# The last stage's matmuls on pairs of fp16 parts instead of pairs of fp32r parts, in one layer of a hybrid attention backbone

## What is computed

```python
def _merge(x, oa, za, ob, zb, ga, gb, gate, w_br_a, w_br_b, w_out):
    ya = (oa * jax.nn.silu(za)) @ w_br_a
    yb = (ob * jax.nn.silu(zb)) @ w_br_b
    h = jax.nn.sigmoid(ga) * ya + jax.nn.sigmoid(gb) * yb
    return x + gate * (h @ w_out)
# and, for both groups of tokens: y = rmsnorm(_merge(...)) * gain
```

## Time and profile before

| | before |
|---|---|
| median of three runs (lowest, highest) | 1109.42 us (1109.13, 1110.87) |
| the profiled execution, its own time | 1108.12 us |
| its span, first to last instruction | 1106.0 us |
| mean granted TensorE clock | 0.996 |
| PE busy / PE weight loads / DVE / ACT / POOL, share of the span | 96% / 85% / 69% / 50% / 9% |
| last stage, PE's last 1106.0 - 881 us | 225 us |

### The profile page before, as it was taken

The page is one execution under the profiler, slowest core; times in us unless marked ns, Lnnn a source line. Parts: engine busy times, 40 slices in busy tenths (PEclk is TensorE's granted clock), DMA queues, the critical chain, the costliest instruction groups (busy, mean ns, idle before and its releaser), DMA issues.

```text
span 1106.0 us, 18405 instructions
## 1 busy us (share of the span) xinstructions
PE 1063.2 (96%) x6515; PEld 941.7 (85%) x6515; DVE 768.0 (69%) x1538; ACT 555.5 (50%) x1036; POOL 104.9 (9%) x115
## 2 busy tenths in 40 slices
PE   5999999999999999998999999989999899999997
PEld 4899888988988898888888888778887789899896
DVE  3669577867876786776788688688688776445443
ACT  4552347645653664565577477377466542212111
POOL 0000200000000000000000000000000165352430
PEclk9999999999999999999999999999999999999999
DMA  9826637964974797399498498669769995353530
GB/s 372 327 84 178 199 88 149 184 189 87 183 160 134 158 190 187 73 192 213 140 184 169 95 177 175 145 138 184 164 144 210 259 337 196 104 195 108 191 134 38
DMA packets 318862, 188.98 MB, mean 171 GB/s; under 512 B 255926, under 2 KB 298934, under 8 KB 317756
## 3 DMA queue, kind: packets, MB, share of 16 engines
q1 hardware_dynamic: 304812, 165.90, 62.0%
q10 hardware_dynamic: 13968, 22.03, 6.0%
HBM read 94.27 MB, written 32.78 MB: 115 GB/s over the span
## 4 chain that ended last, share of the span: by engine, by line
PE 62%; DVE 15%; DMA 8%; ACT 6%; SPq 6%; issue 4%; DVEq 0%; ACTq 0%
PE d_ps_pairs L108 15%; PE y_ps L2157 10%; PE s_ps_pairs L108 10%; PE b_ps L108 10%; PE o_ps_pairs L998 5%; PE v_ps L108 4%; SPq L1130 4%; DMA xl<-pl 4%; DVE pl L1698 4%; DVE mn L1621 3%; ACT pr L1384 2%; DMA xh<-ph 2%; ACT ph L1404 2%; PE s_ps_pairs L1255 1%; PE v_ps L398 1%
## 5 line engine op out<-in xcount | busy, mean ns | idle before, releaser
L108 PE MATMUL d_ps_pairs<-h,wt 128*128 128x384 f32 (+4 forms) x1848 | 353.6, 347 | 3.8 <-ACT craw L1422 3.0
L108 PEld LDWEIGHTS d_ps_pairs<-h,wt 128*128 128x128 f32 x1848 | 320.3, 189 | 26.8 <-issue 5.8
L108 PE MATMUL s_ps_pairs<-h,wt 128*128 128x512 f32 (+1 forms) x864 | 172.5, 357 | 0.0
L1384 ACT ACTIVATE pr<-s_ps_pairs,mx 128x896 f32<-128x896 f32 (+1 forms) x128 | 124.8, 978 | 79.4 <-DVE mx L1643 79.2
L108 PEld LDWEIGHTS s_ps_pairs<-h,wt 128*128 128x128 f32 x864 | 142.6, 190 | 22.0
L1698 DVE SCALAR_TENSOR_TENSOR pl<-pr,rden,ph 128x896 f16<-128x896 f32 (+1 forms) x128 | 140.2, 1116 | 26.7 <-DMA xl<-pl 17.3
L1404 ACT ACTIVATE ph<-pr,rden 128x896 f16<-128x896 f32 (+1 forms) x128 | 124.9, 1011 | 5.5 <-issue 2.7
L2157 PE MATMUL y_ps<-wo,mg 128*128 128x512 f32 (+1 forms) x504 | 113.2, 385 | 0.0
L2157 PEld LDWEIGHTS y_ps<-wo,mg 128*128 128x128 f32 x504 | 91.4, 188 | 20.5
L1621 DVE TENSOR_REDUCE mn<-s_ps_pairs 128x2 f32<-128x1024 f32 x64 | 78.1, 1221 | 26.9 <-PE s_ps_pairs L1258 23.9
L108 PE MATMUL b_ps<-og,wb 128*128 128x256 f32 x720 | 87.8, 282 | 0.2 <-DVE tp L2250 0.2
(11 more groups left out here) (229 smaller groups left out, 1620.8 us busy)
## 6 DMA issues: line engine op xcount, KB each, us to landing
wraw<-in_w_gate SPq DMA_DIRECT2D x24, 512.0 KB, 4.4
gt<-gates_d SPq DMA_DIRECT2D x34, 256.0 KB, 4.9
wada<-in_w_mod SPq DMA_DIRECT2D x6, 1024.0 KB, 10.4
gates_d<-craw ACTq DMA_DIRECT2D x30, 192.0 KB, 3.1
oz<-gates_d SPq DMA_DIRECT2D x20, 256.0 KB, 4.8
oz<-o_d SPq DMA_DIRECT2D x20, 256.0 KB, 4.2
x_f<-in_x SPq DMA_DIRECT2D x10, 512.0 KB, 6.1
y<-y_f SPq DMA_DIRECT2D x9, 512.0 KB, 2.7
```

The costliest lines, as they stand in the source:

```text
L108: mm = eng.matmul(out, lhs(a, k), rhs(b, k), start=(k == 0 and i == 0), stop=(k == n_k - 1 and i == 2))
L1384: act.activation(probs_run(s, t, pb * STEPS + s), scores_run(s, t), ACT.Exp, bias=mx[:, t:t + 1], scale=-1.0, accum_out=den[:, t:t + 1]).t ...
```

## The change

All four operands of the last stage's matmuls become pairs of fp16 parts. For their range each is scaled by a factor made from a largest magnitude found at run time.

- **Largest magnitudes.** For both weights: 32 loads of a half of a weight row block (128x512 fp32, 256 KB) into a free tile `gap_a`, one in each step s = 1 to 8 of branch A, issued by SP behind the step's transposes (`load_half`), and for each a reduction on DVE behind `lower` of the next step (`weights_max`, tile pre). For the gates: in `times_linear` a reduction of the gate just made (24 times, tile vmax); `g_done` is now signalled by it.
- **Factors.** At the start of branch B two small reductions (`all_maxima`); in pair 0 of branch B a transpose and a small matmul on PE, in a part of a PSUM bank that is free there, and some ten operations of a few elements on DVE (`maxima_over_partitions`, `all_factors`). The result is the tile fac.
- **Uses.** The weight splits take their factor as a scale (ACT) and as the scalar of a SCALAR_TENSOR_TENSOR in the place of a TENSOR_TENSOR (DVE). The gate product takes `OF_SUMS` in the place of `sc`. ACT scales the merged sum by 2^-24. The result's factor goes into the product with the adaLN gate, again a SCALAR_TENSOR_TENSOR for a TENSOR_TENSOR.
- **Moved.** The low part of the merged sum goes from POOL to DVE (`merged_low`, one block behind the products), 40 times.
- The tiles of the first two branch weights lie elsewhere; the last two splits of the shared stage buffer in branch B's last pair write them directly.

```diff
+            def load_half(hh):
+                m, h = hh // 2, hh % 2
+                src = io["w_br"][m] if m < KD else io["w_out"][:, m - KD, :]
+                if hh > 0:
+                    sp.wait_ge(pre_max, hh)
+                sp.dma_start(half_raw[:, :], src[:, h * 512:(h + 1) * 512]).then_inc(pre_in, 16)
...
                 turn(s, 1)
+                if A and s >= 1:
+                    load_half(p * SAMPLES + s - 1)
...
                 dve.scalar_tensor_tensor(out=slot, in0=slot, scalar=1.0, in1=d_ps[:, before % 2, 0:n],
-                                         op0=ALU.add, op1=ALU.mult).then_inc(g_done, 1)
+                                         op0=ALU.add, op1=ALU.mult).then_inc(lin_done, 1)
+                if at == 0:
+                    dve.wait_ge(scale, 2)
+                dve.wait_ge(lin_done, at + 1)
+                dve.tensor_reduce(vmax[:, at:at + 1], slot, AX.X, ALU.max, apply_absolute_value=True).then_inc(g_done, 1)
+
+            def weights_max(hh):
+                dve.wait_ge(pre_in, (hh + 1) * 16)
+                dve.tensor_reduce(pre[:, hh:hh + 1], half_raw[:, :], AX.X, ALU.max, apply_absolute_value=True).then_inc(pre_max, 1)
...
+            if not A and p == 0:
+                all_maxima()
...
+                    if p == 0 and s - 3 == MAXIMA_AT:
+                        maxima_over_partitions()
+                    if p == 0 and s - 3 == SPREAD_AT:
+                        all_factors()
...
+                if A and s >= 1 and p * SAMPLES + s >= 2:
+                    weights_max(p * SAMPLES + s - 2)
...
-    dve.tensor_tensor(weight(f, m, 1), weight_raw(f, m), weight(f, m, 0).bitcast(F32), ALU.subtract
-                      ).then_inc(f["w_lo"], 1)
+    dve.scalar_tensor_tensor(out=weight(f, m, 1), in0=weight_raw(f, m), scalar=f["fac"][:, OF_BRANCH if m < KD else OF_OUT],
+                             in1=weight(f, m, 0), op0=ALU.mult, op1=ALU.subtract).then_inc(f["w_lo"], 1)
...
-                pool.wait_ge(mg_hi, i * KD + j + 1)
-                pool.tensor_tensor(mg[1][:, j, :], tp[j % 2][:, 0, :], mg[0][:, j, :].bitcast(F32), ALU.subtract
-                                   ).then_inc(mg_lo, 1)
...
+        def merged_low(i, j):
+            dve.wait_ge(mg_hi, i * KD + j + 1)
+            dve.scalar_tensor_tensor(out=mg[1][:, j, :], in0=tp[j % 2][:, 0, :], scalar=f["fac"][:, OF_MERGED],
+                                     in1=mg[0][:, j, :], op0=ALU.mult, op1=ALU.subtract).then_inc(mg_lo, 1)
...
+                if j > 0 and not (first and j == 1):
+                    merged_low(i, j - 1)
...
-        own_f["mg"].append(sb(ctx, f"mg{n}", [P, KD, CT], F32R))
+            own_f["mg"].append(sb(ctx, f"mg{n}", [P, KD, CT], F16))
...
-        own_f["og"] = sb(ctx, "og", [P, PIECES, 2, 2, CT], F32R)
+        own_f["og"] = sb(ctx, "og", [P, PIECES, 4, 2, CT], F16)[:, :, 0:2, :, :]
```

More of the change, by code:

```diff
@@ L39 @@
 UP = 32768.0
+HALF_UP = 16384.0
+SUM_DOWN = 2.0 ** -24
 ALU = mybir.AluOpType
@@ L809, in pairs @@
     g_ps = o_ps[:, 1, :]
+    f_ps = o_ps[:, 1, 2 * P:4 * P]
+    pre, mx3, half_raw = tiles["pre"], tiles["mx3"], tiles["half"]
+    PRE, SCALED, FACTORS = 32, 7, 11
+    MAXIMA_AT, SPREAD_AT = 1, 3
+    pre_in, pre_max = counts["pre_in"], counts["pre_max"]
     vmax, ones, gm, g1, vs, gs, sc = (tiles[n] for n in ("vmax", "ones", "gm", "g1", "vs", "gs", "sc"))
@@ L983, in weighted @@
             pe.wait_ge(o_done, n - 1)
+        if not A and p == 0 and s == MAXIMA_AT + 2:
+            pe.wait_ge(scale, SCALED + 3)
+        if not A and p == 0 and s == SPREAD_AT + 2:
+            pe.wait_ge(scale, SCALED + 6)
         if s == 0 and A:
@@ L1001, in weighted @@
                                skip_group_check=True)
+        if not A and p == 0 and s == MAXIMA_AT:
+            pe.wait_ge(scale, SCALED + 2)
+            mm = pe.transpose(f_ps[0:3, 0:P], mx3[:, 0:3], ident[:, :])
+        if not A and p == 0 and s == SPREAD_AT:
+            pe.wait_ge(scale, SCALED + 4)
+            mm = pe.matmul(f_ps[:, 0:3], ones[0:3, :], mx3[0:3, 4:7], start=True, stop=True)
         mm.then_inc(pv_done, 1)
@@ L1425, in tile_high @@
             def tile_high(n):
-                i = SPLITS[n][0] if not (last and n == 3) else 2
+                i = SPLITS[n][0]
                 act.wait_ge(w_in, (p * TILES + BEFORE + n + 1) * 16)
@@ L1435, in tile_high @@
                 act.wait_ge(sem, value)
+                if last and n >= 2:
+                    act.wait_ge(scale, SCALED + FACTORS)
+                    act.activation(f["wb"][n - 2][:, 0, :], wraw[:, :], ACT.Copy, scale=f["fac"][:, OF_BRANCH]).then_inc(w_hi, 1)
+                    return
                 act.activation(wt[:, SLOT[i], 0, :], wraw[:, :], ACT.Copy, scale=KEY_SCALE if A and i == 1 else 1.0
@@ new lines, in weights_max, with all_maxima @@
+            def weights_max(hh):
+                dve.wait_ge(pre_in, (hh + 1) * 16)
+                dve.tensor_reduce(pre[:, hh:hh + 1], half_raw[:, :], AX.X, ALU.max, apply_absolute_value=True).then_inc(pre_max, 1)
+            def all_maxima():
+                weights_max(PRE - 1)
+                dve.wait_ge(pre_max, PRE)
+                dve.wait_ge(g_done, UNIT0[PAIRS])
+                dve.tensor_reduce(mx3[:, 0:2], pre[:, :].rearrange("p (w h) -> p w h", w=2), AX.X, ALU.max).then_inc(scale, 1)
+                dve.tensor_reduce(mx3[:, 2:3], vmax[:, 0:silus(UNIT0[PAIRS])], AX.X, ALU.max).then_inc(scale, 1)
@@ L1710, in tile_low @@
             def tile_low(n):
-                i = SPLITS[n][0] if not (last and n == 3) else 2
+                i = SPLITS[n][0]
                 dve.wait_ge(w_hi, p * TILES + BEFORE + n + 1)
+                if last and n >= 2:
+                    dve.scalar_tensor_tensor(out=f["wb"][n - 2][:, 1, :], in0=wraw[:, :], scalar=f["fac"][:, OF_BRANCH],
+                                             in1=f["wb"][n - 2][:, 0, :], op0=ALU.mult, op1=ALU.subtract).then_inc(w_lo, 1)
+                    return
@@ L1794 @@
 PIECES = 4
+OF_BRANCH, OF_OUT, OF_SUMS, OF_RESULT, OF_MERGED = (slice(i, i + 1) for i in range(5))
 GSLOTS = 4
@@ L1824, in tile_high_f @@
         act.wait_ge(f["w_lo"], 2)
-    act.activation(weight(f, m, 0), weight_raw(f, m), ACT.Copy).then_inc(f["w_hi"], 1)
+    act.activation(weight(f, m, 0), weight_raw(f, m), ACT.Copy, scale=f["fac"][:, OF_BRANCH if m < KD else OF_OUT]
+                   ).then_inc(f["w_hi"], 1)
 def tile_low_f(dve, f, m):
     dve.wait_ge(f["w_hi"], m - 1)
-    dve.tensor_tensor(weight(f, m, 1), weight_raw(f, m), weight(f, m, 0).bitcast(F32), ALU.subtract
-                      ).then_inc(f["w_lo"], 1)
+    dve.scalar_tensor_tensor(out=weight(f, m, 1), in0=weight_raw(f, m), scalar=f["fac"][:, OF_BRANCH if m < KD else OF_OUT],
+                             in1=weight(f, m, 0), op0=ALU.mult, op1=ALU.subtract).then_inc(f["w_lo"], 1)
 def load_weight(sp, f, io, m):
@@ L2062, in body @@
                 act.wait_ge(summed, i * KD + j + 1)
[L2063 removed]
+                act.activation(mg[0][:, j, :], tp[j % 2][:, 0, :], ACT.Copy, scale=f["fac"][:, OF_MERGED]).then_inc(mg_hi, 1)
                 if first and j == 0:
@@ L2292, in body @@
                     dve.wait_ge(y_mm, i * 4 + 2 * e + n + 1)
-                    dve.tensor_tensor(y[:, e, half], y_ps[:, e, half], gate[:, half], ALU.mult).then_inc(gated, 1)
+                    dve.scalar_tensor_tensor(out=y[:, e, half], in0=y_ps[:, e, half], scalar=f["fac"][:, OF_RESULT],
+                                             in1=gate[:, half], op0=ALU.mult, op1=ALU.mult).then_inc(gated, 1)
                     dve.wait_ge(gated, i * 4 + 2 * e + n + 1)
@@ L2323, in build @@
             ("vmax", [P, 24]), ("ones", [P, P]), ("gm", [P, 1]), ("g1", [P, 1]), ("vs", [P, 1]), ("gs", [P, 1]),
-            ("sc", [P, 1]))}
+            ("sc", [P, 1]), ("pre", [P, 32]), ("mx3", [P, 8]), ("fac", [P, 8]), ("mul3", [P, 8]))}
         with ExitStack() as cached:
@@ L2374, in build @@
                 ("vc16", [P, 8, 2, HD], F16), ("gap", [P, 512], F32), ("comb", [P, 2, NB + 2 * EDGE], F32))}
+        tiles["half"] = own_a["gap"]
         with ExitStack() as region:
@@ L2394, in build @@
             own_f["gt_first"] = sb(early, "gt_first", [P, KD - EARLY_GATES, 2, CT])
-        wo += [sb(ctx, f"wo{k}", [P, 2, D], F32R) for k in range(6, KD)]
+        wo += [sb(ctx, f"wo{k}", [P, 4, D], F16) for k in range(6, KD)]
         own_f.update({n: sb(ctx, n + "_f", shape) for n, shape in (
```

56 lines of the change are left out of this document (40 added, 16 removed).

## The result

The changed kernel took 1123.45 us (median of 4 runs, 1119.86 to 1123.89), the kernel before beside it 1109.28 (4 runs); the ratio is 1.012, with a 95% interval of 1.0095 to 1.0145. It is slower, by 14 us. The profiled execution took 1123.89 us, its span is 1121.8 us against 1106.0.

A forecast was written before the change was run, and what follows sets the result against it. PE was taken to bound the last stage, with an equally long loop through ACT and DVE in branch A. 1108.1 - 16.5 + 20.9 + 4 + 1 = 1117.5 us profiled, so median 1119; 8-in-10 range 1104 to 1131.

The forecast's parts named there:

- Two loops in branch A: Branch A: beside PE, a loop through ACT and DVE takes 7.82 us per step; both added reductions lengthen it by 1.21.
- The first rival: Branch A: DVE's idle time hides the reductions, 1094 us; chance 0.08, or 0.2 together with the half-hidden case at 1106.
- Branch A's 20.9 us: Added reductions delay branch A's four pairs by 6.5, 7.7, 4.3 and 2.4 us, which add to 20.9.
- The margins at the ends of the pairs: Branch A: PE's slack at a pair's end absorbs 0.76 us in pairs 0 and 1, 1.8 in pair 2.
- The loads, 4 us: Branch A: weight halves land 3.5 us after issue; reductions wait 0.3 us in 13 steps, 4 us in all.
- the late bound: Branch A: loads land after 4.9 us; reductions wait 0.6 x 16 + 1.7 x 13, softened by half to 16 us.
- The last stage, 17.1 us before losses: Last stage: fp16 matmuls save 10.3 us at 256 columns and 6.8 at 512, together 17.1; net gain 16.5.
- The first chunk, 0.6 us, bounds 0 and 2: Last stage, first chunk: new DVE work of 3.3 us delays the last weight split, which has 1.7 margin; cost 0.6 us.
- The scaled forms, nothing: ScalarE's and DVE's scaled forms replace unscaled ones on the same elements and cost nothing.
- Merged low halves on DVE, no cost in later chunks: Last stage, chunks 1 to 4: eight merged low halves of 0.418 us fit DVE's idle half and cost nothing.
- Branch B, 1 us: Branch B: pair 0's ten small operations cost 1 us, bounds 0 and 2; the reductions at its start are covered.

The follow-up runs named there:

- run 1: Changed kernel without any run-time maximum: no weight-half loads, no reductions of weights or gate products, constant magnitudes; 1096.4 us, ratio 0.9891 to the kernel before.
- run 5: Kernel before with only the VectorE work added: 24 gate-product reductions and one 512-column reduction in each of branch A's 32 steps; 1134.69 us, ratio 1.0237.
- Run 4: Changed kernel with the 32 loads of weight halves kept but not their 32 reductions, constant weight magnitude; 1109.14 us, ratio 1.001 to the kernel before.
- run 6: Changed kernel, second chunk's first two pieces gated one weight split earlier, its last two loaded ahead of the x rows; 1121.84 us, ratio 1.0142.
- run 10: Changed kernel with sums of squares on ScalarE (last one late), earlier gating and piece loads, residual gate row loaded before the last two weight loads; 1099.06 us, ratio 0.9913.
- run 11: Changed kernel, maxima still on VectorE, with earlier gating and piece loads and the residual gate row loaded before the last two weight loads; 1119.64 us, ratio 1.0108.
- run 2: Changed kernel without the 24 gate-product reductions (constant 40), weight loads and reductions kept; 1108.56 us, ratio 1.0001 to the kernel before.
- run 3: Changed kernel without the 32 weight loads and their 32 reductions (constant 0.25), gate reductions kept; 1105.44 us, ratio 0.9972 to the kernel before.
- run 12: Kernel before with earlier gating and piece loads and the earlier residual gate row load in the last stage, as a control; 1107.65 us, ratio 1.0002.

## Why the prediction was right, and where not

The direction and the mechanism were right: 1119 forecast, 1123.45 measured, and the time goes where it was said to go. Term by term:

- **Two loops in branch A.** Shown. The step grew by the two reductions, 1.21 us forecast, 9.05 - 7.82 = 1.23 measured, and runs 1 and 5 take the loss away and bring it back whole. The first rival (the reductions hidden, DVE being idle for 31% of the span) fell with run 5: an engine that is idle for almost a third of the time can still be the one whose next instruction is late.
- **Branch A's 20.9 us.** Undersized: 22.9 and the 0.6 ahead of the first minimum, 23.5 measured. The minima show by how much in each pair: the distance from pair 0's first minimum to its last grew by 7.6 us (forecast 6.5, with the 0.76 of margin given back), pair 1's by 8.05 (7.7), pair 2's by 5.9 (4.3), pair 3's by 2.0 (2.4). The margins at the ends of the pairs, 0.76, 0.76 and 1.8, were given back only in the third case, and there 0.75 of it; from pair 0 to pair 1 another 0.3 was lost.
- **The loads, 4 us.** Wrong as forecast, small in fact. In the timeline above the reduction of `pre` follows the low half without a wait, no wait of DVE from 160 to 560 us names these loads, and they land 3.0 to 3.2 us after their issue (I took 3.5): no reduction waited for one. Run 4 finds 1.1 us of A's time at most in the transfers. (The forecast's 16 us at the late bound counted 16 + 13 = 29 of the 32 loads.) With the gate reduction ahead of the first minimum, branch A cost 23.5 where the two terms together gave 24.9.
- **The last stage, 17.1 us before losses.** 256 columns: 0.1092 forecast, 20.96/192 = 0.1092 measured (the chain's row at 990.82). 512 columns: 0.220 forecast, 20.72/96 = 0.2158 measured, so this term was 8.8 us and not 6.8. My estimate from three distances was too coarse. TensorE: Matmul & The Clock Gate (the Trainium skill), section Back-to-back issue gap, has N/2.4 + 2.5 ns for the isolated gap of a warm matmul, that is 216 ns; the trace's 0.2158 us agrees with it, here for a run of 96.
- **The first chunk, 0.6 us, bounds 0 and 2.** This is the step that failed. I had put the price of DVE's later work on the last weight split, which PE reached with margin, and overlooked the next thing behind it on DVE's queue: the gating of the second chunk's pieces, on which a buffer, a load and GpSimd depend. The output matmuls, shorter by 1.7 us, also reach the end of their run before these loads have landed. It cost 4.7 us, 3.0 of waiting and 1.7 at the lower granted clock behind it, for which the forecast had no term. Runs 6, 10 and 11 show that path: with the pieces early the stall moves to the residual gate row (3.8 us), with both early it is 0.8 us in run 10 and 1.4 in run 11. The stage's net gain was 12.9 instead of 16.5.
- **The scaled forms, nothing.** Not quite so. A weight split takes 1.28 us on DVE instead of 1.21 and 1.14 on ACT instead of 1.05, the high half of the merged sum 0.51 instead of 0.42, DVE's product with the residual gate 0.75 instead of 0.69. Steady chunks don't show it, since PE has no gap in them; what part it has in the later gating of the second chunk is not shown.
- **Merged low halves on DVE, no cost in later chunks.** Shown: steady chunks last 41.68 us with PE's runs back to back, though one costs 0.53 us on average and not 0.418.
- **Branch B, 1 us.** 1.1 measured; but kernels with the factors' operations there on DVE lie between 310.2 and 314.2 (the changed kernel and runs 2, 3, 4, 6 and 11), and those without them between 310.3 and 313.1 (the kernel before and runs 5 and 12), so this says nothing.

The sum on the profiled execution was short by 6.4 us (1123.9 against 1117.5). By stretches: up to the end of branch A 27.0 us were lost and 24.9 forecast, 2.1 more, which is 3.5 of varying start, 2.6 of reductions and the 4.0 of loads off; from A's end to B's last step 1.7 against 1.0, 0.7 more; the last stage gave 12.9 instead of 16.5, 3.6 more: 4.1 for the stall (4.7 against 0.6), some 1.4 since the first chunk's branch matmuls gained only 0.65 us of their 192 x 0.0107 = 2.1 (PE waits 0.65 and 2.35 us there for transposes of branch B's last step, 0.46 and 0.80 before), less 2.0 for the shorter output matmul. The second of these waits in the changed kernel:

```profile
909.03 0.27 PE L1009 MATMUL o_ps_pairs<-xh,vc_b 128*128 128x256 f16 x1 [2.35 <-DMA xl<-pl]
```

That the median came out 4.5 us from the forecast is in part luck: the loads, forecast at 4 us, cost almost nothing, and that made up for more than half of what the stall and branch A took above their terms.

## What to carry to other kernels

Before adding work to an engine with idle time, follow the loop that it closes with the others for one step, and count every instruction between its last input and its next output. Work like this belongs on the engine whose slack lies beside the loop: here ScalarE took 56 passes with PE full again, and a looser bound by sums of squares did where the maximum was dear. When an engine's work moves later, look past the first consumer to everything behind it on its queue: buffers that are freed there set when loads go out, and the load took 7.65 us here. When a wait of PE is priced, look at the granted clock behind it too.
